# One copy, one turn and one add for the 16 modulation items of an attention stage, instead of one of each per item

## The reference, cut to what matters

```python
def ada_mods(cvec, w, b):
    m = jax.nn.silu(cvec) @ w + b
    return jnp.split(m[:, None, :], 6, axis=-1)
def modulate(h, shift, scale):
    return h * (1.0 + scale) + shift
```

## Time and profile before

| | us |
|---|---|
| median of 3 runs | 3231.95 |
| the three runs | 3223.11 to 3233.7 |
| the profiled execution, time | 3247.25 |
| the profiled execution, span | 3245.4 |
| PE busy, share of the span | 2767.4, 85% |
| DVE busy | 1812.4, 56% |
| ACT busy | 1226.3, 38% |
| POOL busy | 405.2, 12% |
| mean granted TensorE clock | 0.901 of full |

### The profile page before, as it was taken

One profiled execution on the slowest core, in us unless ns is written; L12 is line 12 of the kernel. 1 busy time (PEld: TensorE's weight loads), 2 busy tenths in 40 slices (PEclk: granted clock), 3 DMA queues, 4 the chain that ended last, 5 costly groups with the idle time before them and its releaser, 6 DMA issues.

```text
span 3245.4 us, 56853 instructions
## 1 busy us (share of the span) xinstructions
PE 2767.4 (85%) x23422; PEld 2053.2 (63%) x23422; DVE 1812.4 (56%) x2834; ACT 1226.3 (38%) x1792; POOL 405.2 (12%) x511
## 2 busy tenths in 40 slices
PE   7968896999978979997888888879967889977995
PEld 5746554777766336783777756767755546755773
DVE  3545445444452164444677763479965365546985
ACT  2423333222222116323222222267744227534773
POOL 1000001000001020001444301011111040011111
PEclk9958888999999879996999988899987879988997
DMA  4225661222221000100000021089982100016995
GB/s 168 79 97 182 208 208 63 80 78 103 78 91 59 17 1 1 66 1 20 4 4 4 4 118 57 40 333 399 395 322 92 57 1 2 19 65 239 405 390 198
DMA packets 63488, 384.83 MB, mean 119 GB/s; under 512 B 7825, under 2 KB 7841, under 8 KB 26897
## 3 DMA queue, kind: packets, MB, share of 16 engines
q1 hardware_dynamic: 41792, 292.60, 24.1%
q0 software_dynamic: 21456, 88.82, 7.1%
HBM read 344.65 MB, written 36.70 MB: 118 GB/s over the span
## 4 chain that ended last, share of the span: by engine, by line
PE 69%; DVE 9%; issue 5%; DVEq 4%; ACT 4%; PEld 3%; DMA 3%; PEldq 1%; POOL 1%; ACTq 1%; POOLq 0%; SPq 0%
PE psum L395 14%; PE psum L586 12%; PE psum L2921 5%; PE psum L2023 4%; PE psum L1179 3%; PE psum L1728 3%; PE psum L2942 3%; PE psum L2582 2%; PE psum L1198 2%; PE psum L1189 2%; PEld psum L2921 2%; PE psum L1647 2%; PE psum L1009 2%; PE psum L984 1%; PE psum L377 1%
## 5 line engine op out<-in xcount | busy, mean ns | idle before, releaser
L395 PE MATMUL psum<-arena_r 128*128 128x512 f32 (+1 forms) x888 | 294.2, 360 | 9.8 <-DVE weight_slots_r L420 4.4
L586 PE MATMUL psum<-arena_r 128*128 128x512 f32 x704 | 252.0, 399 | 27.4 <-DVE weight_slots_r L671 13.8
L395 PE MATMUL psum<-arena_r,weight_slots_r 128*128 128x512 f32 (+1 forms) x696 | 249.0, 358 | 0.0
L395 PE MATMUL psum<-h_t_r,arena_r 128*128 128x512 f32 (+1 forms) x616 | 226.7, 368 | 0.3
L586 PE MATMUL psum<-arena_r,weight_slots_r 128*128 128x512 f32 x528 | 208.8, 395 | 0.0
L2023 PE MATMUL psum<-x_t 64*64 64x64 f32 x5376 | 181.3, 220 | 31.7 <-DVEq L2204 15.5
L415 ACT ACTIVATE arena_r<-weight_slots 128x1024 fp32r<-128x1024 f32 x73 | 76.4, 1057 | 343.6 <-PE psum L395 257.5
L2023 PEld LDWEIGHTS psum<-x_t 64*64 64x64 f32 x5376 | 167.0, 135 | 43.5 <-DVEq L2204 20.5
L395 PEld LDWEIGHTS psum<-arena_r 128*128 128x128 f32 x888 | 163.2, 189 | 47.4 <-issue 21.2
L2893 DVE TENSOR_TENSOR weight_slots_r<-weight_slots,arena_r 128x2048 fp32r<-128x2048 f32 x78 | 177.8, 2289 | 26.8 <-ACT arena_r L2888 26.3
L586 PEld LDWEIGHTS psum<-arena_r 128*128 128x128 f32 x704 | 133.2, 191 | 66.8 <-issue 32.1
(11 more groups left out here) (422 smaller groups left out, 5800.8 us busy)
## 6 DMA issues: line engine op xcount, KB each, us to landing
weight_slots<-in_weights SPq DMA_DIRECT2D x277, 1024.0 KB, 7.2
y_rows<-arena POOLq DMA_DIRECT2D x50, 512.0 KB, 8.1
h_rows<-arena POOLq DMA_DIRECT2D x10, 512.0 KB, 2.9
x_keep<-x_t POOLq DMA_DIRECT2D x1, 3072.0 KB, 9.2
x_t<-x_keep POOLq DMA_DIRECT2D x1, 3072.0 KB, 15.3
x_t<-in_x POOLq DMA_DIRECT2D x1, 2048.0 KB, 9.6
arena<-in_cmp_w POOLq DMA_DIRECT2D x1, 2048.0 KB, 7.9
out_x<-x_t SPq DMA_DIRECT2D x1, 2048.0 KB, 7.2
```

The source lines that it names most:

```text
L395: last = self.nc.tensor.matmul(self.bank(n), w[:, kt, :], self.operand(part, kt, a, b), start=(i == 0), stop=(i == len(passes) - 1))
L586: last = nc.tensor.matmul(bank, w(p, k), x(q, k), start=(k == j == 0), stop=(k == n - 1 and j == 2))
```

## The change: what it does, and its diff

The two columns of the silu now stand at columns 30 and 31 of a field of 64 zeros, one field for each of the eight contraction tiles. Item `r` of a stage (0 to 15) takes the 32 columns that begin at 30 - 2`r` of the field, so that its two rows land at partitions 2`r` and 2`r` + 1 of each strip and the other 30 rows add zero. All 16 items of a stage accumulate in bank 1: the first matmul of item 0 starts the group and the last of item 15 stops it. `copy`, `turn` and `move` are then done once in a stage, behind its last unit. The selector `ada_sel` becomes four stacked 32 x 32 identities, so one turn of two matmuls of 128x128 by 128x32 gives the 32 columns of all 16 items. `move` is two additions of 128 x 32 elements. The drain that frees the slot stays with each item.

```diff
@@ Attention.tensor
                     self.ada.products(pe, self.ada_at + u)
-                    if self.ada_at + u:
-                        self.ada.turn(pe, self.ada_at + u - 1)
-                    if self.ada_at + u == self.ada.n - 1:
-                        self.ada.turn(pe, self.ada_at + u)
@@ behind the last unit
                 turn(hk, hk < self.hk - 1)
+            self.ada.turn(pe, self.ada_at // self.ada.PER)
@@ Attention.scalar
-                if self.ada is not None:
-                    self.ada.copy(act, self.ada_at + u)
...
+            self.ada.copy(act, self.ada_at // self.ada.PER)
@@ Attention.vector
-                if self.ada is not None and self.ada_at + units[v][2]:
-                    self.ada.move(dve, self.ada_at + units[v][2] - 1)
...
-            if self.ada_at + self.hk * self.per == self.ada.n:
-                self.ada.move(dve, self.ada.n - 1)
+            self.ada.move(dve, self.ada_at // self.ada.PER)
@@ AdaBeside
+    PER = 16
     def products(self, pe, i):
         w = self.kern.slot_ready(pe, self.first + i).rearrange("p (k c) -> p k c", k=KT)
-        if i >= 2:
-            pe.wait_ge(self.copied[0], self.copied[1] + i - 1)
+        r = i % self.PER
+        if r == 0 and i:
+            pe.wait_ge(self.copied[0], self.copied[1] + i // self.PER)
         for half in (0, 1):
             for j in range(4):
                 kt = 4 * half + j
-                last = self.nc.tensor.matmul(self.bank(i)[32 * j:32 * j + 32, 0:256], self.c_pad[:, kt, :], w[:, kt, :],
-                                             start=(half == 0), stop=(half == 1))
-        last.then_inc(self.summed[0], 1)
+                last = self.nc.tensor.matmul(self.kern.psum[32 * j:32 * j + 32, 1, 0:256],
+                                             self.c_pad[:, half, 64 * j + 30 - 2 * r:64 * j + 62 - 2 * r], w[:, kt, :],
+                                             start=(r == half == 0), stop=(r == self.PER - 1 and half == 1))
+        if r == self.PER - 1:
+            last.then_inc(self.summed[0], 1)
         pe.drain().then_inc(self.tally.sem("weights_used"), 1)
-    def turn(self, pe, i):
+    def turn(self, pe, g):
...
-            last = self.nc.tensor.matmul(self.kern.psum[:, 5, 2 * half:2 * half + 2],
-                                         self.rows(i)[:, half * P:(half + 1) * P], self.kern.const("ada_sel", 0, 2),
+            last = self.nc.tensor.matmul(self.kern.psum[:, 5, 32 * half:32 * half + 32],
+                                         self.kern.ada_rows[:, 0, half * P:(half + 1) * P], self.kern.const("ada_sel", 0, 32),
                                          start=True, stop=True)
...
+    def move(self, dve, g):
+        dve.wait_ge(self.turned[0], self.turned[1] + g + 1)
+        at = g * self.PER
+        for half in (0, 1):
+            b = self.biases[:, 2 * at:2 * (at + self.PER)].rearrange("p (r h s) -> p r h s", h=2, s=1)[:, :, half, :]
+            dst = self.mods[:, 4 * at:4 * (at + self.PER)].rearrange("p (r h s) -> p r h s", h=2, s=2)[:, :, half, :]
+            src = self.kern.psum[:, 5, 32 * half:32 * half + 32].rearrange("p (r s) -> p r s", s=2)
+            last = self.nc.vector.tensor_tensor(out=dst, in0=src, in1=b.broadcast_to([P, self.PER, 2]), op=ALU.add)
+        last.then_inc(self.moved[0], 1)
@@ Silu
-        self.nc.vector.tensor_tensor(out=self.padded[:, :, 0:2], in0=self.x, in1=self.tmp, op=ALU.mult)
+        for a in (0, 1):
+            self.nc.vector.tensor_tensor(out=self.padded[:, a, :].rearrange("p (k c) -> p k c", c=64)[:, :, 30:32],
+                                         in0=self.x[:, a], in1=self.tmp[:, a], op=ALU.mult)
@@ Kernel
-ARENA = 24000
+ARENA = 23968
-        self.c_pad = self.h_t[:, 2, 0:256].rearrange("p (k c) -> p k c", k=KT)
+        self.c_pad = self.h_t[:, 4:6, 0:256]
@@ host
-    ada_sel = np.zeros((P, 2), np.float32)
-    for j in range(4):
-        ada_sel[32 * j, 0] = ada_sel[32 * j + 1, 1] = 1.0
+    ada_sel = np.tile(np.eye(32, dtype=np.float32), (4, 1))
```

More of the change, by code:

```diff
@@ L1621, in __init__ @@
         self.c_pad, self.mods, self.biases = c_pad, mods, biases
-        self.per_layer = 6 * D // 256
         self.n = units
@@ L1625, in __init__ @@
         k.tally.claim("weights_used", units)
[L1626 to L1629, removed]
+        stages = units // self.PER
+        self.summed = self.count("ada_summed", stages)
+        self.copied = self.count("ada_copied", stages)
+        self.turned = self.count("ada_turned", stages)
+        self.moved = self.count("ada_moved", stages)
     def count(self, name, n):
         return self.tally.sem(name), self.tally.claim(name, n)
[L1634 to L1638, removed]
     def products(self, pe, i):
         w = self.kern.slot_ready(pe, self.first + i).rearrange("p (k c) -> p k c", k=KT)
-        if i >= 2:
-            pe.wait_ge(self.copied[0], self.copied[1] + i - 1)
+        r = i % self.PER
+        if r == 0 and i:
+            pe.wait_ge(self.copied[0], self.copied[1] + i // self.PER)
         for half in (0, 1):
@@ L1650, in products @@
+        if r == self.PER - 1:
+            last.then_inc(self.summed[0], 1)
         pe.drain().then_inc(self.tally.sem("weights_used"), 1)
-    def turn(self, pe, i):
-        pe.wait_ge(self.copied[0], self.copied[1] + i + 1)
-        if i >= 1:
-            pe.wait_ge(self.moved[0], self.moved[1] + i)
+    def turn(self, pe, g):
+        pe.wait_ge(self.copied[0], self.copied[1] + g + 1)
+        if g:
+            pe.wait_ge(self.moved[0], self.moved[1] + g)
         for half in (0, 1):
-            last = self.nc.tensor.matmul(self.kern.psum[:, 5, 2 * half:2 * half + 2],
-                                         self.rows(i)[:, half * P:(half + 1) * P], self.kern.const("ada_sel", 0, 2),
+            last = self.nc.tensor.matmul(self.kern.psum[:, 5, 32 * half:32 * half + 32],
+                                         self.kern.ada_rows[:, 0, half * P:(half + 1) * P], self.kern.const("ada_sel", 0, 32),
@@ L1659, in turn, with copy @@
                                          start=True, stop=True)
         last.then_inc(self.turned[0], 1)
[L1662 to L1674, removed]
+    def copy(self, act, g):
+        act.wait_ge(self.summed[0], self.summed[1] + g + 1)
+        if g:
+            act.wait_ge(self.turned[0], self.turned[1] + g)
+        self.nc.scalar.activation(self.kern.ada_rows[:, 0, :], self.kern.psum[:, 1, 0:256], ACT.Copy).then_inc(self.copied[0], 1)
@@ L3228, in block_one @@
         self.mod = [vec[:, i * 96:(i + 1) * 96].rearrange("p (m s) -> p m s", s=2) for i in (0, 1)]
-        Silu(self, self.cond.rearrange("p (k s) -> p k s", s=2), self.cond_sig.rearrange("p (k s) -> p k s", s=2), self.c_pad)
+        Silu(self, *(y.rearrange("p (a k s) -> p a k s", a=2, s=2) for y in (self.cond, self.cond_sig)), self.c_pad)
         mix = Norm(self, x, h, KT, KT, segs, lambda t, a: c("norm_mix", t), c("ones_1024", 0, P))
@@ L3266, in block_one @@
         self.attention_buffers(work_at, SEQ)
-        ada = AdaBeside(self, self.c_pad, self.mod, [c("ada_b", layer * 48, 48) for layer in (0, 1)], 48)
+        ada = AdaBeside(self, self.c_pad, vec[:, 0:192], c("ada_b", 0, 96), 48)
         Attention(self, 96, SEQ, 4, 1, 4, lambda hh, t: heads[0:96, hh, bass.ds(t * P, P)],
```

## The result

The median of three runs is **3186.87 us** (3179.17 to 3189.4) against 3231.95: ratio 0.986, 95% interval 0.9813 to 0.9907. The profiled execution took 3189.4 us with a span of 3187.6 and a mean granted clock of 0.904 (before: 3247.25, 3245.4, 0.901).

The account below looks back on a forecast made before the run. TensorE was taken to bound the kernel. Turns removed, 22.7 us, less 1.5 at the stage ends and 0.3 at the start, gave 20.9 us saved: 3211 us from 3231.95, with an 8-in-10 range of 3196 to 3225.

Parts of the forecast that it names:

- Turns removed: Item stages: of 48 turns, 43 save 0.44 us at full clock, three 0.80, the last two together 1.37; sum 22.7 us.
- The gap behind the products: TensorE's 0.29 us idle after each item's products was to stay, as in the one unit without a turn.
- Copies and adds cost nothing: Removing 45 ScalarE copies and 45 VectorE adds was costed at nothing, both engines idling over half of each item stage.
- the ring's 285 GB/s: Item units of 3.68 us need 285 GB/s of transfers; the rival of a 263 GB/s limit, 3228 us, had chance 0.04.
- L1637's 110 ns: The products' shifted weight loads were to stay at 110 ns; the rival of slower loads, 3253 us, had chance 0.03.
- TensorE as the bound: In the item stages TensorE was to stay the limit after the change, with full-clock units of 3.68 us.
- Stage ends, 1.5 us: Added tail behind each stage's last unit: 0.56 us for each of the first two stages, 0.36 for the third.
- The arena's 32 columns cost nothing: Cost at the start: shrinking the arena by 32 columns was taken as free.
- The clock: Rival that half-clock stretches move in the item stages; each unit changing level costs or gives about 3 us.
- the late case: Clock rival: a stage starts with three slow units, 9 us, giving 3222 to 3228 us; chance 0.10.
- the early one: Clock rival: stages one and three rise at their first item, gaining 14 us, giving 3197 us; chance 0.08.
- The removed turns stream only two columns each, so the remaining work is denser: Reason given for full clock starting sooner in the item stages: about 4.5 units gain 3 us; chance 0.08.

Follow-up runs that it names:

- the first study: Kernels before and after unchanged, and after with dummy matmuls of 2 or 128 columns put back per unit; before 3233.09 us, after 3189.14 us.
- The two single versions: Kernel after with its arena moved to 122880 (3226.11 us), and kernel before with only the arena address of after (3220.07 us).
- e3_sparse: Kernel after with two dummy matmuls of 2 columns per unit where the turn's stood, no waits; 3193.19 us, ratio 0.9866.
- e5_layout: Kernel before with constants padded and the arena 32 columns smaller, so the arena starts at 122752 as in after; 3220.07 us, ratio 0.9945.
- e15_all_zero: Kernel before with a 128-byte spacer and padded constants, so slots, `x`, `h_t` and arena start at multiples of 256 bytes; 3209.35 us, ratio 0.993.
- e13_change_alone: Kernel after with 36 more columns of constants, so the arena starts at 122880, a multiple of 256 as before; 3226.11 us, ratio 0.9966.

## Why the prediction was wrong

**The account.** The clock-free time fell by 2926.0 - 2889.4 = 36.6 us, and the half-clock time by 617 - 598 = 19 us, worth 9.5. Together 46 us, against 44 in the medians of the first study. By cause: 22 us of shorter item stages; 18 of aligned buffers, which came by luck; 9.5 of clock, which neither part owns. These add up to 49.5, so 3 to 4 us are counted twice or lost elsewhere. The two single versions sum to 25.4 + 18.3 = 43.7, 7 us more than both together. Both gaps stay open.

**Point by point.**

- *Turns removed, 22.7 us; net 20.9*: right. The unit is 3.65 us, the loads of the turn are 12, and the stages give 22 us. The gap behind the products stays, as said. But a change of tiling and the kernel's drain are at most half of it: dummies that also take the whole array, with no wait ahead, start 0.13 us earlier (`e3_sparse`).
- *Copies and adds cost nothing*: right; the ring's 285 GB/s, L1637's 110 ns, TensorE as the bound: right. No wait for a slot appears in the units shown.
- *Stage ends, 1.5 us*: too high. By the end of stage two it is about 0.2 us a stage, at most 0.6 in all; the pair of adds takes 0.28 us together, and part of what followed L1092 had been there before.
- ***"The arena's 32 columns cost nothing"*: the step that failed.** I counted the bytes of the constants and the size of the arena, and never looked at where the arena starts. 120 bytes more of constants moved it from 122624 to 122752. This gave 18 us of clock-free time (13 us of median in `e5_layout` and 21 in `e15_all_zero`, each against the kernel before beside it). It was luck: in `e13_change_alone` the arena stands another 128 bytes further on, the 231.2 ns are back, and the clock-free time is 11 us longer than after's. (The constants grew by 1.5%, not 1.6%, which changes nothing.)
- *The clock*: named as the widest unknown, and rightly, but priced in the wrong place. I priced units that change level in item stages, at 9 us for the late case and 14 for the early one. Stages one and three did rise earlier and stage two rose later. The stage with the greatest swing, 18 us, was one that I had not looked at. "The removed turns stream only two columns each, so the remaining work is denser" has no support: 2 and 128 columns give the same clock, and the change alone has more half-clock time than the kernel before beside it (644 and 607 us), not less.
- *The rule of the Trainium skill*, "TensorE: Matmul & The Clock Gate", section What's actually happening, that sustained activity releases the throttle, is no help for these stretches: PE was busy 31.54 of 33.80 us at 0.50, and 48.71 of 51.50 at 0.57.
- *The range*: two things were left out, addresses and the clock in stages away from the change. With the change alone (3226.11) the result would have come out just above the range, with both (3186.87) below it.

## What to carry to other kernels

An edit that changes a buffer's size can move every buffer behind it: compare the addresses, and run the old kernel with the new layout, before a gain is put down to the edit. Matmuls that leave TensorE's queue give their start-to-start distance. A fulfilled wait that leaves it gives something only if no other wait takes its place behind the drain. Where the clock has two levels, compare time x mean granted clock beside the median, and never take the difference of two profiled executions for the gain.

## What the runs showed of the hardware

- Float32r matmuls of 128x512 come every 227.2 ns when the buffers that hold their operands start at the same place modulo 256 bytes (two layouts), and every 230.3 to 232.4 ns in the six other layouts tried; the cause isn't shown.
- One kernel, on one layout, stands 565 to 677 us of 3200 at half clock, and the same code (the WKV preparation) can run mostly at half clock in one execution (51.5 us at 0.57) and mostly at full in the next (33.2 us at 0.93).
- Two fulfilled waits on TensorE's queue behind a drain cost 0.12 to 0.13 us; one alone was not measured.
- A stationary slice of 32 columns at any even offset from 0 to 30 loads in a median of 110 ns (768 loads), as one at a fixed place does.
